# Expert weights of a mixture layer: four landing buffers, shared buffers for the rounded parts, one engine for the down rest

## The reference

```python
h = _layer_norm(DN_ALPHA * h + mixed, ln1_g[li], ln1_b[li])
ff = _hier_moe(h, ...)      # 32 experts, each token goes to 2 of them

# in _hier_moe: the 2 * 1040 (token, expert) pairs sorted by expert, in blocks of 128 rows
xb = h[row_tok].reshape(n_blocks, MOE_BLOCK, D)          # D = 1024
def expert_block(args):
    xe, e = args
    return (jax.nn.silu(xe @ w1[e]) * (xe @ w3[e])) @ w2[e]   # w1, w3: 1024x256, w2: 256x1024
yb = lax.map(expert_block, (xb, block_e)).reshape(n_rows, D)
y = jnp.zeros((T, D), jnp.float32).at[row_tok].add(yb * row_gate[:, None])
```

## Time and profile before

| | |
|---|---|
| median of 3 runs | 5523.99 us (5523.89 to 5526.87) |
| span of the profiled execution | 5519.8 us, first to last instruction |
| TensorE busy in the span | 4898.7 us, 89% |
| VectorE busy | 3334.8 us, 60% |
| ScalarE busy | 2133.5 us, 39% |
| GpSimd busy | 1683.3 us, 30% |
| granted TensorE clock, mean | 0.946 |

### The profile page before, as it was taken

How to read it: one execution, slowest core, us unless ns; L and a number is a source line. 1 busy time by engine, 2 the same in 40 slices (tenths; PEclk the granted TensorE clock), 3 DMA queues, 4 the chain that set the end, 5 groups by cost and what they waited for, 6 DMA issues and landing times. The chain is left out here.

```text
span 5519.8 us, 128974 instructions
## 1 busy us (share of the span) xinstructions
PE 4898.7 (89%) x56564; PEld 4170.6 (76%) x56564; DVE 3334.8 (60%) x5051; ACT 2133.5 (39%) x3885; POOL 1683.3 (30%) x1036
## 2 busy tenths in 40 slices
PE   6989999998799956989999998799966998999999
PEld 5888888886577746878888886577755766788887
DVE  5435655558688864345655557688865455563552
ACT  2323333332277752333333332177753234232331
POOL 0013322222277740012332222177741100022221
PEclk9999999998799987989999998799987998999999
DMA  4410101013366653410101004266653101233333
GB/s 131 140 50 19 31 19 29 20 29 110 104 227 229 233 182 101 133 52 18 31 20 30 19 18 118 93 226 229 227 182 121 35 5 54 88 97 121 111 92 111
DMA packets 383085, 536.30 MB, mean 97 GB/s; under 512 B 136482, under 2 KB 306594, under 8 KB 354466
## 3 DMA queue, kind: packets, MB, share of 16 engines
q1 hardware_dynamic: 339714, 488.61, 27.8%
q0 software_dynamic: 41472, 34.21, 2.1%
q10 hardware_dynamic: 1344, 5.24, 0.3%
HBM read 573.01 MB, written 122.09 MB: 126 GB/s over the span
## 5 line engine op out<-in xcount | busy, mean ns | idle before, releaser
L267 PE MATMUL ps<-w,xbT 128*128 128x512 f32 x2304 | 570.6, 405 | 89.5 <-DVE w L2399 89.5
L2399 DVE TENSOR_TENSOR w<-w,w 128x2048 fp32r<-128x2048 f32 x192 | 545.5, 2868 | 75.2 <-ACT w L2356 75.2
L267 PEld LDWEIGHTS ps<-w,xbT 128*128 128x128 f32 x2304 | 439.3, 194 | 193.0 <-DVE w L2399 101.4
L267 PE MATMUL ps<-hT,w_in 128*128 128x416 f32 (+1 forms) x2736 | 490.9, 338 | 9.0 <-DVE w_in L748 9.0
L267 PEld LDWEIGHTS ps<-hT,w_in 128*128 128x128 f32 x2736 | 457.7, 195 | 34.9 <-issue 28.9
L1473 POOL TENSOR_TENSOR lm<-Ab,consts 116x416 f32<-116x416 f32 x240 | 254.5, 1068 | 611.7 <-PE ps L267 334.8
L2356 ACT ACTIVATE w<-w 128x2048 fp32r<-128x2048 f32 x192 | 362.6, 1937 | 97.5 <-DMA w<-in_moe_w_dram,widx 97.5
L267 PE MATMUL ps<-v,pT 104*104 104x128 f32 (+1 forms) x2176 | 274.2, 283 | 28.2 <-issue 27.4
L267 PE MATMUL ps<-w,actT 128*128 128x512 f32 x1152 | 278.4, 390 | 5.8 <-POOL w L2348 3.0
L267 PEld LDWEIGHTS ps<-v,pT 104*104 104x104 f32 (+1 forms) x2176 | 252.8, 181 | 40.0 <-issue 32.3
L2348 POOL TENSOR_TENSOR w<-w,w 128x1024 fp32r<-128x1024 f32 x96 | 268.6, 2798 | 29.1 <-ACT w L2392 27.6
(11 more groups left out here) (445 smaller groups left out, 11222.9 us busy)
## 6 DMA issues: line engine op xcount, KB each, us to landing
w<-in_moe_w_dram SPq DMA_DIRECT2D x192, 1024.0 KB, 8.2
w_gate<-in_w_gate_dram SPq DMA_DIRECT2D x44, 512.0 KB, 3.8
w_up<-in_w_up_dram SPq DMA_DIRECT2D x44, 512.0 KB, 3.8
w_down<-in_w_down_dram SPq DMA_DIRECT2D x44, 512.0 KB, 3.2
w_in<-in_w_in_dram SPq DMA_DIRECT2D x36, 512.0 KB, 4.4
ys<-t_ys SPq DMA_DIRECT2D x20, 832.0 KB
t_h<-x SPq DMA_DIRECT2D x30, 416.0 KB
w_out<-in_w_out_dram SPq DMA_DIRECT2D x24, 512.0 KB, 7.6
```

Of the source, the lines that this page charges most:

```text
L267: made = e.matmul(out, a, b, start=start, stop=stop)
L2399: e.tensor_tensor(w.lo, w.x, w.hf, ALU.subtract).then_inc(*P.c("moe_dve").tick(li, "w13", b, k))
```

## The change

- The landing places of the weights are separated from the places of the rounded parts. There are four landing buffers for the up weights and four for the down weights (`NL` = 4, buffer b % 4), in which x arrives and lo is left, and two buffers of hi for each (b % 2). The memory in all is the same: 4 x 4096 + 2 x 4096 against 3 x 8192 words a partition for the up weights.
- The loads of block b wait for block b-4 in place of b-3. GpSimd issues the gathers of an overflow block one block further ahead. The routing step loads blocks 0, 1 and 3.
- Since overflow blocks now use all four buffers, plain and indirect loads have semaphores of their own (`w`, `g`), 24 names where there were 9. Four of them share a semaphore with the embedding stage.
- GpSimd makes no rest of the down weights. VectorE makes all of it, in one operation of 128 x 2048.

```diff
-NB, NX = 3, 5
+NL, NX = 4, 5
-    m.w13 = [P.split(2, 2048, "w13") for _ in range(NB)]
-    m.w2 = [P.split(1, 2048, "w2") for _ in range(NB)]
+    m.w13_in = [P.landing(2, 2048, "w13") for _ in range(NL)]
+    m.w13_hi = [P.rounded(2, 2048, "w13_hi") for _ in range(2)]
+    m.w2_in = [P.landing(1, 2048, "w2") for _ in range(NL)]
+    m.w2_hi = [P.rounded(1, 2048, "w2_hi") for _ in range(2)]
+def up_weights(P, b):
+    (x, lo), hi = P.moe.w13_in[b % NL], P.moe.w13_hi[b % 2]
+    return Split(hi, hi.bitcast(F32), lo, x)
...
 def moe_first(e, P, li):
-    for b in range(NB - 1):
-        moe_up_load(e, P, li, b)
-        moe_down_load(e, P, li, b)
+    for b in range(NL):
+        if not gathered(b):
+            moe_up_load(e, P, li, b)
+            moe_down_load(e, P, li, b)
...
 def moe_sp(e, P, li):
-    for b in range(NB, NBLK):
-        if b % NB != 2:
-            e.wait_ge(*pe.at(li, "up", b - NB))
+    for b in range(NL, NBLK):
+        if not gathered(b):
+            e.wait_ge(*pe.at(li, "up", b - NL))
             moe_up_load(e, P, li, b)
...
     for b in range(NX - 1):
         rows_in(b)
+        if b < NL - 1:
+            load(b)
+            load2(b)
     for b in range(NBLK + 2):
-        if b + NB - 1 < NBLK:
-            load(b + NB - 1)
+        if b + NL - 1 < NBLK:
+            load(b + NL - 1)
...
-        if b and b + 1 < NBLK:
-            load2(b + 1)
-        if b < NBLK:
-            w, c = m.w2[b % NB], slice(0, 1024)
-            e.wait_ge(*ac.at(li, "w2", b))
-            e.tensor_tensor(w.lo[:, 0, c], w.x[:, 0, c], w.hf[:, 0, c], ALU.subtract).then_inc(*po.tick(li, "w2", b))
+        if 1 <= b < NBLK - 2:
+            load2(b + 2)
...
 def moe_dve(e, P, li):
-            w, c = m.w2[b % NB], slice(1024, 2048)
+            w = down_weights(P, b)
             e.wait_ge(*ac.at(li, "w2", b))
-            e.tensor_tensor(w.lo[:, 0, c], w.x[:, 0, c], w.hf[:, 0, c], ALU.subtract).then_inc(*dv.tick(li, "w2", b))
+            e.tensor_tensor(w.lo, w.x, w.hf, ALU.subtract).then_inc(*dv.tick(li, "w2", b))
...
 def moe_pe(e, P, li):
-            e.wait_ge(*po.at(li, "w2", p))
             e.wait_ge(*dv.at(li, "w2", p))
```

More of the change, by code:

```diff
@@ L169 @@
 SHARED.update({f"com_{s}_in": f"sp_w{8 + s}_in" for s in range(4)})
+SHARED.update({f"moe_w1{s}_in": f"emb_x{s}_in" for s in range(4)})
 SHARED.update({f"clo_m{s}_in": f"sp_w{8 + s}_in" for s in range(3)})
@@ L238, in split, with landing, rounded @@
         return Split(view(1, F32R), view(1, F32R).bitcast(F32), view(0, F32R), view(0, F32))
+    def landing(self, a, b, name):
+        o = (self.top + 7) // 8 * 8
+        self.top = o + a * b
+        assert self.top <= SB, self.top
+        return [self.place(o, a * b, dt, name).rearrange("p (a b) -> p a b", b=b) for dt in (F32, F32R)]
+    def rounded(self, a, b, name):
+        o = (self.top + 7) // 8 * 8
+        self.top = o + a * b
+        assert self.top <= SB, self.top
+        return self.place(o, a * b, F32R, name).rearrange("p (a b) -> p a b", b=b)
     def pair(self, width, name):
@@ L2104, in route_pool @@
     m, po = P.rt, P.c("moe_pool")
-    e.memset(P.moe.w13[2].x, 0.0).then_inc(*po.tick(li, "zero", 0))
-    e.memset(P.moe.w2[2].x, 0.0).then_inc(*po.tick(li, "zero", 1))
+    e.memset(up_weights(P, 2).x, 0.0).then_inc(*po.tick(li, "zero", 0))
+    e.memset(down_weights(P, 2).x, 0.0).then_inc(*po.tick(li, "zero", 1))
     for s in range(NX):
@@ L2239, with gathered @@
 ROUTE = ("rt_dve", "rt_act", "rt_pe")
-NB, NX = 3, 5
+NL, NX = 4, 5
+def gathered(b):
+    return b % 3 == 2
 def table_column(b):
-    return NEXP + b // NB if b % NB == 2 else 2 * (b // NB) + b % NB
+    return NEXP + b // 3 if gathered(b) else 2 * (b // 3) + b % 3
 def moe_mem(P):
@@ new lines, in moe_mem, with down_weights, weights_in @@
+    m.w13_hi = [P.rounded(2, 2048, "w13_hi") for _ in range(2)]
[4 more added lines that the diff above has]
+    return Split(hi, hi.bitcast(F32), lo, x)
+def down_weights(P, b):
+    (x, lo), hi = P.moe.w2_in[b % NL], P.moe.w2_hi[b % 2]
+    return Split(hi, hi.bitcast(F32), lo, x)
+def weights_in(P, k, b):
+    return P.d(f"moe_{'g' if gathered(b) else 'w'}{k}{b % NL}_in")
@@ L2292, in moe_sp @@
             moe_up_load(e, P, li, b)
-        if b > NB and (b - 1) % NB != 2:
-            e.wait_ge(*pe.at(li, "down", b - 1 - NB, 1))
+        if b > NL and not gathered(b - 1):
+            e.wait_ge(*pe.at(li, "down", b - 1 - NL, 1))
             moe_down_load(e, P, li, b - 1)
@@ L2305, in moe_pool, with gather @@
     e.wait_ge(*po.at(li, "zero x", NX - 1))
-    def gather(out, table, idx, bound, sem, *event):
+    def gather(out, table, idx, bound, into, b):
         e.indirect_dma_start(out, None, table, bass.IndirectOffsetOnAxis(idx, 0), bounds_check=bound, oob_is_err=False
-                             ).then_inc(*P.d(sem).tick(li, *event))
+                             ).then_inc(*into.tick(li, b))
     def rows_in(b):
@@ L2313, in rows_in @@
             e.wait_ge(*pe.at(li, "xT", b - NX, 1))
-        gather(m.xb[b % NX], T["h"], P.toks[:, table_column(b):table_column(b) + 1], L - 1, f"moe_x{b % NX}_in", b)
+        gather(m.xb[b % NX], T["h"], P.toks[:, table_column(b):table_column(b) + 1], L - 1, P.d(f"moe_x{b % NX}_in"), b)
     def load(b):
[L2317 to L2322, removed]
-    def load2(b):
[L2325 to L2329, removed]
+        o = b // 3
+        if gathered(b):
+            if b >= NL:
+                e.wait_ge(*pe.at(li, "up", b - NL))
+            w = up_weights(P, b).x
+            gather(w[:, 0, :], v1, P.widx[:, o:o + 1], wb, weights_in(P, 1, b), b)
+            gather(w[:, 1, :], v3, P.widx[:, o:o + 1], wb, weights_in(P, 3, b), b)
+    def load2(b):
+        o = b // 3
+        if gathered(b):
+            if b >= NL:
+                e.wait_ge(*pe.at(li, "down", b - NL, 1))
+            gather(down_weights(P, b).x[:, 0, :], v2, P.widx[:, o:o + 1], wb, weights_in(P, 2, b), b)
     for b in range(NX - 1):
         rows_in(b)
+        if b < NL - 1:
+            load(b)
+            load2(b)
     for b in range(NBLK + 2):
-        if b + NB - 1 < NBLK:
-            load(b + NB - 1)
+        if b + NL - 1 < NBLK:
+            load(b + NL - 1)
         if b + NX - 1 < NBLK:
@@ L2396, in moe_weights_dve @@
     for k in range(2):
[L2397 removed]
+        w = up_weights(P, b).at(k)
         e.wait_ge(*P.c("moe_act").at(li, "w13", b, k))
@@ L2464, in moe_pe @@
                     e.wait_ge(*ac.at(li, "yo", p - 1, c))
-                w = [m.w2[p % NB].at(0, slice(1024 * k + 512 * c, 1024 * k + 512 * c + 512)) for k in range(2)]
+                w = [down_weights(P, p).at(0, slice(1024 * k + 512 * c, 1024 * k + 512 * c + 512)) for k in range(2)]
                 mms(e, [x for k in range(2) for x in three(P.ps[5 + c][:, :], m.aT[p % 2].at(k), w[k], k == 0, k == 1)]
@@ L2477 @@
 MOE = ("moe_pe", "moe_dve", "moe_act", "moe_pool", "moe_y0_out", "moe_y1_out") + tuple(
-    f"moe_{x}{s}_in" for s in range(NB) for x in ("w1", "w2", "w3")) + tuple(f"moe_x{s}_in" for s in range(NX))
+    f"moe_{x}{k}{s}_in" for s in range(NL) for x in "wg" for k in (1, 2, 3)) + tuple(f"moe_x{s}_in" for s in range(NX))
 def combine_mem(P):
```

29 lines of the change are left out of this document (14 added, 15 removed).

## The result

| | before | after |
|---|---|---|
| median | 5523.94 us (4 runs) | 5429.4 us (4 runs, 5427.2 to 5434.0) |
| ratio to before | | 0.9829, interval 0.9816 to 0.9842 |
| span of the profiled execution | 5519.8 us | 5427.4 us |
| U(0) to U(47), first and second pass | 495.8, 494.3 us | 449.0, 449.0 us |
| GpSimd busy | 1683.3 us | 1304.0 us |

The change made the kernel faster by 94.5 us; 5430.3 was forecast. U(b) is, as before, the start of block b's first up product.

A forecast was written before the change was run, and what follows sets the result against it. TensorE's waits for late gathers and for VectorE's rests conflicting with GpSimd's cost some 55 us a pass. At 9.58 us per block the passes lose 47.7 and 46.1 us; with -0.8 and +0.9, 5524.0-93.7 = 5430.3 us, range 5411 to 5469.

The forecast's parts named there:

- The loop: Expert stage: ScalarE's copy, VectorE's down rest, xbT rests and up rests set 9.58 us per block, against TensorE's 9.34.
- Rival B: Expert stage: VectorE's loop is slack and TensorE sets the pace at 9.34 us per block, 5408 us; chance 0.08.
- The upper bound of this term: VectorE's loop: at most 9.88 us per block, if both up rests keep their excess of 0.59 us.
- VectorE's conflict with GpSimd: Expert stage: the two engines' rests stop each other; removing GpSimd's takes away 0.59 us per up rest, 1.2 per block.
- the row at 1799.69: VectorE's rest taking 3.92 us instead of 2.28, read as held until GpSimd's rest ended at 1801.45, done 2.28 later.
- Late gathers: Overflow blocks' weight gathers: one block, 9.6 us, more lead covers the largest wait of 4.6 twice; all 28 waits go.
- With them the slow restarts: TensorE's slow up products after a late gather, 7.36 us against 5.73 for 24, vanish along with the waits.
- 5.73 us everywhere: Expected sign: TensorE's 24 up products take 5.73 us in all blocks.
- GpSimd's queue: Only indirect transfers, nine in three blocks, 22 us of 28.7, at worst 28.8; cost 0, bound +0.1 us in three blocks.
- Small terms: Stage ends: U(0) to U(1) stays 7.4 us, semaphores +0.45 and last block -0.4 a pass; DMA share about 0.65.
- The sum: Both passes: -47.7 and -46.1 us, with -0.8 and +0.9 making -93.7 us, so 5430.3 us.
- Rival D: Expert stage: GpSimd's transfers each hold VectorE's rests 1.03 us, 11.06 us per block, 5566 us; chance 0.04.

The follow-up runs named there:

- Half the rest left out: Changed kernel with VectorE making only the second half of the down rest, the first half's products taking the rounded part: 5402.7 us, ratio 0.9775.
- the rest moved out of the loop: Changed kernel with the down weights' rounding and rest moved one step later, behind the up weights of block b+2: 5400.6 us, ratio 0.9774.
- the loads' half alone: Changed kernel's buffers and load lead, but GpSimd keeps its half of the down rest as in the kernel before: 5445.9 us, ratio 0.9858.
- the kernel without any added lead: Kernel before with its three buffer sets and load lead, VectorE making the whole down rest: 5432.4 us, ratio 0.9826.
- another order of VectorE's: Kernel before's three buffers and lead, VectorE making the whole down rest, down weights handled behind block b+2's up weights: 5408.9 us, ratio 0.9792.

## Why the prediction was right

- **The loop.** U(b+2) = U(b)+19.15 was forecast, 19.21 measured. The 0.06 is the down rest: the next operation starts 2.27 us after it, where 2.21 was taken. Half the rest left out, and the rest moved out of the loop, both gave TensorE's pace of 9.34 us, which is what the step claimed. Rival B did not come because the loop is real; there was no hidden slack. The upper bound of this term was worked out wrongly: two rests with an excess of 0.59 us each would make the loop 20.33, which is 10.17 us per block and not 9.88.
- **VectorE's conflict with GpSimd.** Excess of 0.59 us on each up rest, forecast to go: mean 2868 to 2277 ns. Its price, once gathers are on time, is 25 us a pass (the loads' half alone beside half of the rest left out); 13 of them are left as gain after VectorE has taken over the work. The prediction's reading of the row at 1799.69 was off by a little: VectorE was done 2.16 us after GpSimd's rest, not 2.28.
- **Late gathers.** All 28 waits were taken as gone, and they are. The reason was wrong in part, and that the term still came out was in part luck. The step rested on the lead ("9.6 covers it twice") and took the 7.2 us of block 29 as needed ever after; in the changed kernel the second gather lands 1.1 to 1.5 us after its issue, because it is issued ahead of the plain loads. The removal of GpSimd's rest from in front of the gathers was only mentioned. It suffices alone: the kernel without any added lead has the same 449 us. That either half cures the late gathers also explains why the halves do not add up: 79 us for the loads alone, 92 for the rest alone, 95 to 100 for both. "With them the slow restarts" was right too, but only 11 of the 28 late blocks had one. The products of block 0 stay slow, 6.86 and 6.84 us, as they were before; "5.73 us everywhere" did not hold there.
- **GpSimd's queue.** Taken as 0 and right for this kernel. The bound was too low: 2.9 us was my worst transfer, 3.1 occurred here, and 6.8 with another order of VectorE's. The mean was 1.45 us, where 2.16 was taken.
- **Small terms.** U(0) to U(1) 7.5 us (7.4 forecast). The last block's down products came 0.46 and 0.38 us earlier after U(47) (0.4). The 15 added semaphore names were taken as +0.45 us a pass and cost none: from the last down products' start to SyncE's first load it is 6.76 us before and after (2020.34-2013.58, 1972.23-1965.47). The DMA share of the stretch went to 0.62, where about 0.65 was said.
- **The sum.** -46.8 and -45.3 us in the passes, -0.8 at their ends: -92.9, forecast -93.7 with the semaphores. The span fell by 92.4 us.
- **Rival D**, GpSimd's transfers holding VectorE for 1.03 us each, is measured at about 0.04 us, on the down rest only, where a transfer starts with it. In the changed kernel 39 rests of 128x2048 began while a transfer was already running; they average 2.28 us, like the 132 that met none.

## What to carry to other kernels

Where one engine is nearly always busy, write the loop that its waits close, from rows of the trace, and compare it with that engine's own pace: here 19.2 against 18.7 us for two blocks said more than VectorE's total, which did not change. Then move work that is needed late out of that loop, instead of shortening it. An operation ahead of a DMA issue in the same stream can make its data late by more than its own length, when it pushes the issue behind another engine's burst of loads. So compare the time from issue to landing in the late cases with that in the others, see what was issued just before, and try the order before paying for another buffer. A wait can also be for a transfer that moves nothing: look at the bytes.

## What the runs showed of the hardware

- VectorE's operation with two inputs in SBUF (the rests) delays an indirect transfer of GpSimd that begins while it runs. In the changed kernel the 81 transfers that began within 0.03 us of a rest's start took 1.02 to 1.05 us, and those that began with no rest running took 0.97 to 1.03. The 100 that began 0.05 us or more after a rest's start took 1.6 to 3.1 us, and each of them ended 0.86 to 1.08 us after the end of a rest. Most get in between two rests; the one of 6.82 us, once a pass in one kernel, missed both gaps between three. With half of the down rest left out the 288 transfers of a trace averaged 1.05 us, against 1.45 in the changed kernel: only 13 of them began inside a rest there. The Trainium skill ("SBUF — State Buffer", "Who interferes with whom") has such an operation as no cause of stalls for these transfers; the measurement decides.
- In the other direction the same pair hardly meets: VectorE's down rest grows from 2.29 to 2.33 us when a transfer starts with it, and a rest that starts during a transfer takes the same 2.28 us as without one.
- An indirect transfer that moves nothing landed 1.1 us after its issue on a quiet queue, and 6.4 to 8.5 us after it when three plain loads of 1 MB had been issued in the 3 us before.
